# The last quarter of the tokens leaves the dense expert products: its rows are fetched one pick at a time

## The reference, cut to what matters

```python
# h: 512 tokens x 1024; u, v: 16384 experts x 1024; expert, gate: 8 heads x 16 picks = 128 per token
u_sel = u[expert]
v_sel = v[expert]
act = jax.nn.gelu(jnp.einsum('nd,ned->ne', hx, u_sel), approximate=False)
return jnp.einsum('ne,ned->nd', gate * act, v_sel)
```

## Time and profile before

| what | us |
|---|---|
| median of the runs | 2600.27 |
| profiled execution, whole | 2599.47 |
| profiled execution, span from first to last instruction | 2597.4 |
| TensorE busy | 2467.7 (95%) |
| GpSimd busy | 1556.1 (60%) |
| VectorE busy | 1379.4 (53%) |
| ScalarE busy | 594.9 (23%) |

### The profile page before, as it was taken

One profiled execution on the slowest core, in us unless ns is written; L12 is line 12 of the kernel. 1 busy time (PEld: TensorE's weight loads), 2 busy tenths in 40 slices (PEclk: granted clock), 3 DMA queues, 4 the chain that ended last, 5 costly groups with the idle time before them and its releaser, 6 DMA issues. The chain is left out here.

```text
span 2597.4 us, 37806 instructions
## 1 busy us (share of the span) xinstructions
PE 2467.7 (95%) x12856; PEld 1258.9 (48%) x12856; DVE 1379.4 (53%) x2401; ACT 594.9 (23%) x1238; POOL 1556.1 (60%) x1048
## 2 busy tenths in 40 slices
PE   6979989999999999989999999999899898999997
PEld 3435534444555555434444444444357544457743
DVE  6695748999677777129722222240204533554434
ACT  2313211111222222111111111110216332245412
POOL 6763459888776676799866666660570067830063
PEclk8989999999999999999999999999999899999999
DMA  6324443555457857877755656560220022310021
GB/s 262 104 73 162 143 149 125 155 150 153 135 154 240 253 157 237 266 258 265 243 203 201 205 199 207 198 217 17 82 98 1 9 82 94 101 49 1 9 73 49
DMA packets 189246, 375.31 MB, mean 144 GB/s; under 512 B 13664, under 2 KB 79200, under 8 KB 189152
## 3 DMA queue, kind: packets, MB, share of 16 engines
q1 hardware_dynamic: 119696, 332.54, 38.3%
q10 hardware_dynamic: 69456, 41.50, 5.4%
HBM read 302.68 MB, written 71.30 MB: 144 GB/s over the span
## 5 line engine op out<-in xcount | busy, mean ns | idle before, releaser
L687 PE MATMUL ps<-hT,parts 128*128 128x512 f16 x4800 | 1057.3, 381 | 38.1 <-DVE arena L1397 14.5
L636 POOL TENSOR_SCALAR parts<-ring 128x1024 f16<-128x1024 f32 x261 | 289.3, 1108 | 806.7 <-PE ps L687 781.2
L687 PEld LDWEIGHTS ps<-hT,parts 128*128 128x128 f16 x4800 | 467.2, 98 | 599.2 <-issue 23.4
L687 PE MATMUL ps<-arena 128*128 128x512 f16 x3072 | 668.7, 381 | 6.8 <-DVE arena L1738 6.8
L639 POOL TENSOR_TENSOR parts<-ring,parts 128x1024 f16<-128x1024 f32 x261 | 566.6, 2171 | 21.8
L687 PEld LDWEIGHTS ps<-arena 128*128 128x128 f16 x3072 | 301.5, 98 | 374.9 <-issue 16.8
L1733 DVE TENSOR_TENSOR arena<-arena 128x512 f32<-128x512 f32 x128 | 142.3, 1112 | 438.2 <-DMA arena<-gate_mem 435.2
L657 POOL TENSOR_TENSOR arena<-ring,arena 128x1024 f16<-128x1024 f32 x128 | 283.2, 2213 | 10.6
L637 POOL TENSOR_SCALAR ring<-ring 128x1024 f32<-128x1024 f32 x261 | 281.0, 1077 | 0.0
L655 POOL TENSOR_SCALAR arena<-ring 128x1024 f16<-128x1024 f32 x128 | 147.6, 1153 | 171.6 <-PE ps L687 171.6
L1228 ACT ACTIVATE spare<-ps 128x512 f32<-128x512 f32 x128 | 76.5, 597 | 567.5 <-PE ps L687 421.2
(11 more groups left out here) (171 smaller groups left out, 2257.5 us busy)
## 6 DMA issues: line engine op xcount, KB each, us to landing
ring<-w SPq DMA_DIRECT2D x133, 512.0 KB, 3.3
ring<-u SPq DMA_DIRECT2D x128, 512.0 KB, 3.9
ring<-v SPq DMA_DIRECT2D x128, 512.0 KB, 3.4
act_mem<-spare SPq DMA_DIRECT2D x128, 256.0 KB, 4.0
gate_mem<-arena ACTq DMA_DIRECT2D x4, 8192.0 KB, 43.0
arena<-act_mem SPq DMA_DIRECT2D x128, 256.0 KB, 3.6
arena<-gate_mem SPq DMA_DIRECT2D x128, 256.0 KB, 3.8
arena<-ada_w SPq DMA_DIRECT2D x48, 512.0 KB, 5.6
```

Source lines behind the costliest of these rows:

```text
L636: G.tensor_scalar(dst[:, 0, :], src, WS, 1.0, ALU.mult, ALU.mult).then_inc(scaled, 1)
L687: ins = [T.matmul(out_, a, b, start=start and j == 0, stop=stop and j == 2) for j, (a, b) in enumerate(((lhs[0], rhs[0]), (lhs[0], rhs[1]) ...
```

## The change

The last 128 tokens (`FEW`) leave the dense products, which are then 384 wide (`DENSE`); gates are spread for 48 groups instead of 64, stored in four blocks of 96 tokens. For the 128 tokens, one per partition, each of the 128 picks is one indirect DMA issued by GpSimd: 128 rows of 4 KB, into one of six buffers at the end of `arena` (`fetch`). For a U row VectorE takes the product with the token's h, which TensorE has turned to token rows in two PSUM banks (`turn_few`), and sums it in the same instruction. ScalarE takes the gelu of the 128 x 128 dots, VectorE multiplies with the gates, and for each V row adds gate x act x row to a sum in SBUF (`add_few`). TensorE turns that sum into the output's layout with one fp32 matmul per bank. The expert numbers and gates go to HBM and back.

Work moves between engines. From chunk 100 on (`RAISED`) ScalarE makes two of the three passes over a U tile, and for all V tiles it makes the f16 high part; GpSimd keeps the subtractions. SyncE's loads run five chunks ahead of its stores and pair loads (`U_LEAD`, `V_LEAD`). The V loops of ScalarE, GpSimd and VectorE are written out instead of looped. The squares of one norm lie in `arena` instead of `hT`.

The diff, cut to what carries the change:

```diff
+SET = 128
+SETS = 1
+FEW = SET * SETS
+DENSE = S - FEW
+BATCH = DENSE // 4
+GROUPS = DENSE // GROUP
+SIDES = P // SET
+ROWS_AHEAD = 6
+PER_TILE = 4
+U_LEAD, V_LEAD = 5, 5
 ZG, ZG_HEAD = 10, 5
 AT_EXPS, AT_TURN, AT_GATES = 40, 44, 48
+FETCH = AT_GATES + GROUP
+RAISED = AT_GATES + GROUPS + RING
...
+        fetched_rows = arena[:, ROOM:ROOM + ROWS_AHEAD * D].rearrange("p (a b) -> p a b", a=ROWS_AHEAD)
+        few_idx, few_gate, few_dot = (root[:, j * FEW:(j + 1) * FEW] for j in range(3))
+        fold = root[:, 3 * FEW:3 * FEW + SET]
...
+            return hT[:, 2 * j:2 * j + 2, :].rearrange("p a b -> p (a b)")
...
+        def fetch_chunk(k):
+            return 112 * k // FEW
...
+            for c in range(U_LEAD):
                 load(T_EXP + c, u_in[c])
-            with sp.Fori(0, (CHUNKS - GROUP) // RING) as it:
+            with sp.Fori(0, TAIL // RING) as it:
                 for r in range(RING):
                     c = it * RING + r
-                    load(T_EXP + GROUP + r, tile_of(u_in, c + GROUP), it)
+                    load(T_EXP + U_LEAD + r, tile_of(u_in, c + U_LEAD), it)
...
+                    load(S_V + V_LEAD + r, tile_of(v_in, it * 4 + (V_LEAD + r)), it)
...
+            def cut_raised(n):
+                pool.wait_ge(raised, 2 * (n - T_EXP - RAISED + 1))
+                src, dst = ring[:, n % RING, :], parts[:, n % RING, :, :]
+                G.tensor_tensor(dst[:, 1, :], src, dst[:, 0, :], ALU.subtract).then_inc(parts_ready, 1)
+            def fetch(n):
+                if n >= ROWS_AHEAD:
+                    wait_apart(rows_used, n - ROWS_AHEAD + 1)
+                rows = u_rows_in if n < FEW else v_in.rearrange("c p n -> (c p) n")
+                at = n % FEW
+                G.indirect_dma_start(
+                    out=fetched_rows[:, n % ROWS_AHEAD, :], out_offset=None, in_=rows,
+                    in_offset=bass.IndirectOffsetOnAxis(ap=few_idx[:, at:at + 1].bitcast(U32), axis=0),
+                ).then_inc(rows_fetched[n % ROWS_AHEAD], 16)
...
-            def cut_v(c, it=0):
-                if c >= 2 * GROUP:
-                    pool.wait_ge(down, it * 2 * GROUP + (c - 2 * GROUP + 1))
-                wait_apart(loaded[(S_V + c) % RING], it * 64 + 16 * ((S_V + c) // RING + 1))
+                    cut_tile(n, n + ahead, 0, raised_by_act)
+            def cut_v(c):
+                pool.wait_ge(v_high, c + 1)
...
-                G.tensor_scalar(dst[:, 0, :], src, 1.0, 1.0, ALU.mult, ALU.mult).then_inc(v_high, 1)
...
+            cut_tiles(RING, T_EXP + FETCH, 0)
+            pool.wait_ge(pick_loaded, 16 * 2 * SIDES)
+            for n in range(ROWS_AHEAD):
+                fetch(n)
+            cut_tiles(T_EXP + FETCH, T_EXP + RAISED, 0)
+            n = ROWS_AHEAD
+            for c in range(RAISED, CHUNKS):
+                for _ in range(PER_TILE):
+                    if n < FEW:
+                        fetch(n)
+                        n += 1
+                cut_raised(T_EXP + c)
+            while n < FEW + ROWS_AHEAD:
+                fetch(n)
+                n += 1
+            for c in range(CHUNKS):
+                while n < 2 * FEW and fetch_chunk(n - FEW) <= c:
+                    fetch(n)
+                    n += 1
                 cut_v(c)
...
+                                        (hi[:, 0:DENSE], lo[:, 0:DENSE]), k == 0, k == KC - 1)
...
+            def turn_few(j):
+                first = DENSE + j * SET
+                for k in range(KC):
+                    for side in range(SIDES):
+                        for h, half in enumerate(hr(k)):
+                            mm = T.matmul(few_rows(j)[side * SET:(side + 1) * SET, k * P:(k + 1) * P],
+                                          half[:, first:first + SET], ident_h, start=(h == 0), stop=(h == 1))
+                mm.then_inc(few_turned, 1)
...
+            ups(AT_GATES + GROUPS, AT_GATES + GROUPS + 4)
...
+            pe.wait_ge(rows_used, FEW)
...
+            pe.wait_ge(rows_used, 2 * FEW)
...
+                    mm = T.matmul(ps[:, o, at:at + SET], few_sum(j)[:, o * P:(o + 1) * P], fold, start=True, stop=True)
...
+            gelus(AT_EXPS, AT_TURN)
+            act.wait_ge(pick_ready, 1)
+            act.dma_start(pick_mem[0], pick_row[P - FEW:P, :]).then_inc(pick_stored, 16)
+            act.dma_start(pick_mem[1], chosen[P - FEW:P, NT - 1, 2, :]).then_inc(pick_stored, 16)
+            gelus(AT_TURN, AT_GATES)
+            act.wait_ge(pick_stored, 32)
+            for j, dst in enumerate((few_idx, few_gate)):
+                for q in range(SIDES):
+                    rows = pick_mem[j][:, q * SET:(q + 1) * SET].rearrange("(s t) k -> t s k", s=SETS)
+                    act.dma_start(dst[q * SET:(q + 1) * SET, :].rearrange("p (s k) -> p s k", s=SETS),
+                                  rows).then_inc(pick_loaded, 16)
...
+            def raise_tile(n):
+                act.wait_ge(loaded[n % RING], 16 * (n // RING + 1))
+                src = ring[:, n % RING, :]
+                A.activation(parts[:, n % RING, 0, :], src, ACT.Copy, scale=WS).then_inc(raised, 1)
+                A.activation(src, src, ACT.Copy, scale=WS).then_inc(raised, 1)
+            for c in range(AT_GATES + GROUPS, CHUNKS):
+                gelu_chunk(c % 4, c)
+                if RAISED <= c + RING - 1 < CHUNKS:
+                    raise_tile(T_EXP + c + RING - 1)
+            act.wait_ge(rows_used, FEW)
+            A.activation(few_dot, few_dot, ACT.Gelu).then_inc(few_gelu, 1)
...
+            def v_tile_high(c):
+                if c >= 2 * GROUP:
+                    act.wait_ge(down, c - 2 * GROUP + 1)
+                act.wait_ge(loaded[(S_V + c) % RING], 16 * ((S_V + c) // RING + 1))
+                A.activation(v_parts[:, c % (2 * GROUP), 0, :], ring[:, (S_V + c) % RING, :],
+                             ACT.Copy).then_inc(v_high, 1)
+            for i in range(2):
+                act.wait_ge(gates_out[i], 16 * (DENSE // BATCH) // 2)
+            for c in range(V_LEAD):
+                v_tile_high(c)
+            for c in range(CHUNKS):
+                high(c % (2 * GROUP), c)
+                if c + V_LEAD < CHUNKS:
+                    v_tile_high(c + V_LEAD)
...
+            own.link(V.scalar_tensor_tensor(out=pick_f, in0=chosen[:, NT - 1, 1, :], scalar=float(P),
+                                            in1=chosen[:, NT - 1, 0, :], op0=ALU.mult, op1=ALU.add))
+            own.do(V.tensor_copy(pick_row.bitcast(U32), pick_f), pick_ready)
+            own.link(V.tensor_copy(fold, ident[:, 0:SET]))
...
+            own.do(V.tensor_copy(ident_h, ident[:, :]))
...
+            def await_rows(n):
+                dve.wait_ge(rows_fetched[n % ROWS_AHEAD], 16 * (n // ROWS_AHEAD + 1))
+                return fetched_rows[:, n % ROWS_AHEAD, :]
+            for k in range(FEW):
+                if k % SET == 0:
+                    dve.wait_ge(few_turned, k // SET + 1)
+                row = await_rows(k)
+                V.tensor_tensor_reduce(out=row, in0=row, in1=few_rows(k // SET), scale=1.0, scalar=0.0,
+                                       op0=ALU.mult, op1=ALU.add,
+                                       accum_out=few_dot[:, k:k + 1]).then_inc(rows_used, 1)
...
+            def add_few(k):
+                row = await_rows(FEW + k)
+                w, sums = few_dot[:, k:k + 1], few_sum(k // SET)
+                dve.wait_ge(rows_used, FEW + k)
+                if k % SET == 0:
+                    dve.wait_ge(down, 1)
+                    V.tensor_scalar(sums, row, w, None, ALU.mult).then_inc(rows_used, 1)
+                else:
+                    V.scalar_tensor_tensor(out=sums, in0=row, scalar=w, in1=sums, op0=ALU.mult,
+                                           op1=ALU.add).then_inc(rows_used, 1)
+            k = 0
+            for c in range(CHUNKS):
+                multiply(c % (2 * GROUP), c, c // (2 * GROUP))
                 if c >= 1:
+                    low_part((c - 1) % (2 * GROUP), c - 1)
+                if c == 2:
+                    dve.wait_ge(few_gelu, 1)
+                    own.link(V.tensor_tensor(few_dot, few_dot, few_gate, ALU.mult))
+                while k < FEW and fetch_chunk(k) + 2 <= c:
+                    add_few(k)
+                    k += 1
```

More of the change, by code:

```diff
@@ L253, in build @@
         iota_h = in_x[:, 6 * 512:6 * 512 + P // 2].bitcast(F16)
+        ident_h = in_x[:, 6 * 512 + P // 2:6 * 512 + P].bitcast(F16)
+        assert 2 * CHUNKS * BATCH <= ROOM
         cut = Cut()
         v_parts = cut.parts(2 * GROUP, TILE)
-        w_parts = cut.parts(2 * GROUP, S)
-        pair = cut(4, 2, S)
-        prod = cut(2, S)
+        w_parts = cut.parts(2 * GROUP, DENSE)
+        pair = cut(4, 2, DENSE)
+        prod = c_row[:, 0:2 * DENSE].rearrange("p (a b) -> p a b", a=2)
+        assert cut.at <= ROOM
         cut = Cut()
@@ L660, in _ @@
                 cut_tile(n, n)
[L661 to L664, removed]
+            cut_tiles(RING, T_EXP + FETCH, 0)
```

(30 more changed lines are left out.)

101 lines of the change are left out of this document (60 added, 41 removed).

## The result

The changed kernel takes 2707.72 us (median of 4 runs, 2700.03 to 2709.76) against 2599.98: ratio 1.041, interval 1.0388 to 1.0432. Slower by 108 us, where 2507 was forecast. Its span is 2704.9 us.

A forecast was written before the change was run, and what follows sets the result against it. TensorE was taken to set the pace of the expert stage. Gates end at 892, plus 249 U tail, 8 seam, 12 ramp, 528 and 40 V half: 1729 against 1822, gain 93, so 2507 us; own range 2470 to 2555, overall 2430 to 2650.

The forecast's parts named there:

- chunks 0 to 43: U half start: VectorE's routing (top-k) is not shortened and ends at 642; gain 7.5 us of a possible 57.
- the full transfers of the U rows: U chunks 96 to 127: 96.5 MB at 388 GB/s take 249 us, so the U half ends at 1141.
- The seam's sum: Between U and V halves: gelu, ScalarE's first five V passes, GpSimd's first subtraction in a row before TensorE, 8 us.
- V half, 120 chunks: V half: TensorE and transfers 3.9, GpSimd 3.6 to 5.0 with clashes; 4.4 taken, 528 us for 120 chunks.
- a little over the middle: V half: choice of 4.4 us a chunk between 3.6 and 5.0, partly because fetches wait for a row buffer.
- Rival D: V half: row chain (fetch, add, free buffer, fetch) slower than any engine, 5.18 us a chunk; time 2600, chance 0.04.
- Rival C: U tail and V half: GpSimd's price of a fetch makes it slower, time 2699 at 2.13 us; chance 0.22.
- f: GpSimd's time for one indirect fetch of 128 rows, taken as 1.25 us, between 0.33 and 2.13.
- Rival A: U tail and V half: fetches cheap (0.33 us), few clashes, transfers at 419 GB/s; time 2434, chance 0.16.
- Rival B: V half: VectorE and GpSimd take turns in every case, 5.0 us a chunk; time 2579, chance 0.12.
- all clashes: V half: VectorE's operations slow GpSimd, 0 to 1.42 us a chunk on top of its 3.6.

The follow-up runs named there:

- the ring wide: Changed kernel with each V chunk's pair loads issued before the V tile load and seven row buffers instead of six: 2518.33 us, ratio 0.968.

## Why the prediction was wrong

Up to the end of the gates mechanism and sizes were right: what TensorE saves in chunks 0 to 43 is lost to the routing. What it saves later is lost beside the full transfers of the U rows, 398 GB/s where the earlier trace rows gave 388. The V half starts 1.5 us before its forecast, but in part by luck: the dots were done 9 us early and the seam took 15.2 us instead of 8. The seam's sum had GpSimd's first subtraction in it, but not the load that may only start behind it and that ScalarE's fifth V pass waits for: ScalarE stands 6.96 us there.

The step that failed is "V half, 120 chunks". It priced engines and transfers side by side and put the row buffers in as "a little over the middle, since each fetch also waits for a row buffer of VectorE". That wait, the row ring, is the bound, not a rounding. It costs 5.84 - 4.38 = 1.46 us a chunk, 185 us in all, more than the 108 us lost; with the ring wide the kernel is at 2518, 11 us from the forecast and inside its own range of 2470 to 2555. That 4.38 meets the forecast 4.4 is partly luck: the prediction had GpSimd over 90% busy, and in that run GpSimd is busy 371 of 470 us and VectorE 431. Rival D named the row chain but left it at 5.18 a chunk for want of a working, with a chance of 0.04. It could have been worked out from the rows and the diff: fetch 1.25, subtraction 2.17, three issues of 0.33, a landing of 3.8 us (the gate tiles in the page before), product and low part 0.5 each (the earlier trace rows by 3/4), addition 1.4 (the dot of the earlier trace rows): 10.6 us over the 2.25 chunks that the indices give, 4.7 us a chunk at the least, above the 4.4 taken; with the 5.4 us from the issue to VectorE's start in the trip shown it is 5.4.

Rival C is refuted: f is 1.25, the middle that was taken. The Trainium skill, "DMA: Bandwidth & Descriptors", "Latency and other measured facts", gives about 1 us; the trace has 0.94 us busy, and 1.25 from start to start. Rival A fell with it. Rival B is right in kind. With the ring wide the additions cost at least 0.50 us a chunk, where the forecast held 0.8 for all clashes (4.4 less 3.6); beside a subtraction an addition of 1.27 us takes 3.15. The rule that the prediction quotes from the Trainium skill, "SBUF — State Buffer", "Who interferes with whom", agrees with this: the addition of 1509.39 ends 1.1 us after GpSimd's second subtraction (1506.51 + 4.95 = 1511.46). Timeline of the run without V fetches, VectorE and GpSimd:

```profile
1505.32 1.27 DVE L1906 SCALAR_TENSOR_TENSOR hT<-arena,spare,hT 128x1024 f32<-128x1024 f32 x1
...
1506.51 4.95 POOL L722 TENSOR_TENSOR arena<-ring,arena 128x1024 f16<-128x1024 f32 x2 [3.13 <-ACT arena L1397]
...
1509.39 3.15 DVE L1906 SCALAR_TENSOR_TENSOR hT<-arena,spare,hT 128x1024 f32<-128x1024 f32 x1
```

## What to carry to other kernels

When a buffer is freed by an engine that itself waits, through other queues, for the engine that fills it, draw the ring: add up the latencies of one trip and divide by the number of steps that the indices let it advance. It binds although no engine and no transfer is busy over three quarters, and one buffer more (132 us here), or two issues swapped in a queue (135 us), can be worth more than the whole change. Count the latencies as they are at the faster pace: here the trip grew from 13 to 15 us when it was widened. And an engine's saving counts only up to the next bound of its own stretch, here routing, then the stretch with full transfers.

## What the runs showed of the hardware

A fetch of 128 scattered rows of 4 KB occupies GpSimd 0.94 us for U and 0.95 for V (medians; up to 1.76 in the V half), and the next starts 1.25 us after it in the U tail. Such fetches with plain loads beside them run at 382 to 411 GB/s over stretches of 70 to 88 us and at 398 over the whole 240 us, so here scattered rows of this size transfer as well as rows in a line (388 and 419 in the earlier trace rows). TensorE's granted clock fell from 1.00 in the V half before to 0.91 (0.78 with five buffers), where it works a chunk and then stands for some us; it was lower where the stands were longer. The slower clock did not set the pace there: VectorE waited for TensorE once in the V half of the changed kernel, 3.6 us.
